# Three reorderings in a two-layer streaming encoder: modulation tiles behind softmax rows, one spread a third of a projection later, one low part ahead of the rotary key

## The reference

```python
for l in range(DEPTH):                                  # DEPTH = 2
    mod = c_act @ w_ada[l] + b_ada[l]                   # 6 * 1024 numbers from the conditioning vector
    sh1, sc1, g1, sh2, sc2, g2 = split(mod, 6)
    h = x * (1.0 + sc1) + sh1
    z = h @ w_in[l]                                     # one projection for four groups of heads
    a_u, a_v, b_cq, b_ckv, b_kr, c_u, d_q, d_f, d_i, d_g = split(z)
    y_a = spatial_gating(gelu(a_u), gelu(a_v), ...)
    y_b = mla(b_cq, b_ckv, b_kr, ...)                   # latent attention, rotary key, 4 heads
    y_c = s5(c_u, ...)                                  # diagonal state-space model
    y_d = hgrn2(d_q, d_f, d_i, d_g, ...)                # gated linear recurrence in chunks of 64
    x = layer_norm(ALPHA * x + (1 + g1) * (rms(y_a..y_d) @ w_out[l]))
    h = x * (1.0 + sc2) + sh2
    x = layer_norm(ALPHA * x + (1 + g2) * conv_ffn(h, ...))   # width 2816, gated, causal conv of 3
```

## Time and profile before

| | us |
|---|---|
| median of 3 runs | 1355.19 |
| lowest, highest | 1354.09, 1362.82 |
| the profiled execution | 1352.38 |
| its span, first to last instruction | 1350.6 |
| mean granted clock of PE, as a share of 2.4 GHz | 0.978 |

### The profile page before, as it was taken

One profiled execution on the slowest core, in us unless ns is written; L12 is line 12 of the kernel. 1 busy time (PEld: TensorE's weight loads), 2 busy tenths in 40 slices (PEclk: granted clock), 3 DMA queues, 4 the chain that ended last, 5 costly groups with the idle time before them and its releaser, 6 DMA issues.

```text
span 1350.6 us, 17196 instructions
## 1 busy us (share of the span) xinstructions
PE 1298.7 (96%) x6802; PEld 1004.0 (74%) x6802; DVE 904.1 (67%) x1537; ACT 532.5 (39%) x796; POOL 243.6 (18%) x201
## 2 busy tenths in 40 slices
PE   6899999999999999999999999999999999999997
PEld 3445767776788888888876677777778888888886
DVE  5985777856877777758657958575675555553335
ACT  2523223533633334434218443443363333343323
POOL 0640200533300000000029432053330000000003
PEclk9998999999999999999989999989999999999998
DMA  9455643122466666755317151122223233333321
GB/s 389 170 125 172 134 152 102 40 66 91 170 189 191 199 194 196 252 203 188 95 61 201 52 96 50 35 87 68 77 91 97 94 94 98 105 95 94 94 94 63
DMA packets 65232, 170.90 MB, mean 127 GB/s; under 512 B 14336, under 2 KB 27008, under 8 KB 64256
## 3 DMA queue, kind: packets, MB, share of 16 engines
q1 hardware_dynamic: 65152, 169.81, 40.3%
HBM read 162.07 MB, written 7.72 MB: 126 GB/s over the span
## 4 chain that ended last, share of the span: by engine, by line
PE 78%; DVE 14%; DMA 2%; issue 2%; POOL 1%; ACT 1%; SPq 0%; ACTq 0%; POOLq 0%; DVEq 0%
PE bank L558 20%; PE bank L560 20%; PE bank L559 20%; PE bank L681 3%; PE bank L708 2%; PE bank L573 1%; PE bank L675 1%; PE bank L567 1%; PE bank L873 1%; PE bank L836 1%; DVE xa L1275 1%; PE bank L578 1%; DVE xa L1281 1%; PE bank L845 1%; DMA cf<-in_consts 1%
## 5 line engine op out<-in xcount | busy, mean ns | idle before, releaser
L558 PE MATMUL bank<-ym_r,scr_r 128*128 128x512 f32 x688 | 268.7, 391 | 6.4 <-DVE hm_r L1942 4.2
L560 PE MATMUL bank<-hm_r,scr_r 128*128 128x512 f32 x688 | 267.8, 389 | 0.0
L559 PE MATMUL bank<-ym_r,ring_r 128*128 128x512 f32 x688 | 267.8, 389 | 0.0
L1344 DVE TENSOR_TENSOR ring_r<-ring,scr_r 128x1024 fp32r<-128x1024 f32 x134 | 165.5, 1235 | 86.1 <-ACT scr_r L2097 85.9
L2097 ACT ACTIVATE scr_r<-ring 128x1024 fp32r<-128x1024 f32 x146 | 153.4, 1052 | 129.5 <-DMA ring<-in_w_down 105.3
L558 PE MATMUL bank<-scr_r 128*128 128x512 f32 x480 | 188.6, 393 | 2.8 <-DVE ym_r L1876 2.8
L559 PE MATMUL bank<-scr_r,ring_r 128*128 128x512 f32 x480 | 187.4, 390 | 0.0
L558 PEld LDWEIGHTS bank<-ym_r,scr_r 128*128 128x128 f32 x688 | 129.1, 188 | 38.2 <-issue 7.8
L560 PEld LDWEIGHTS bank<-hm_r,scr_r 128*128 128x128 f32 x688 | 129.1, 188 | 26.7
L559 PEld LDWEIGHTS bank<-ym_r,ring_r 128*128 128x128 f32 x688 | 129.1, 188 | 26.6
L2438 ACT ACTIVATE scr<-bank,pb 128x512 f32<-128x512 f32 x86 | 67.0, 779 | 194.9 <-PE bank L560 194.9
(11 more groups left out here) (395 smaller groups left out, 2036.9 us busy)
## 6 DMA issues: line engine op xcount, KB each, us to landing
ring<-in_w_up SPq DMA_DIRECT2D x88, 512.0 KB, 3.6
ada<-in_w_ada SPq DMA_DIRECT2D x80, 512.0 KB, 3.6
ring<-in_w_down SPq DMA_DIRECT2D x44, 512.0 KB, 3.5
ring<-in_w_in SPq DMA_DIRECT2D x33, 512.0 KB, 4.3
scr<-in_w_ada SPq DMA_DIRECT2D x16, 512.0 KB, 14.1
ring<-in_w_out SPq DMA_DIRECT2D x16, 512.0 KB, 3.5
pa<-in_par_a SPq DMA_DIRECT2D x2, 2144.5 KB, 12.7
xa<-in_x SPq DMA_DIRECT2D x1, 2048.0 KB, 8.0
```

What stands on the lines that cost most here:

```text
L558: first = mm(dst, w_hi, x_hi, start=start, stop=False)
L559: mm(dst, w_lo, x_hi, start=False, stop=False)
L560: return first, mm(dst, w_hi, x_lo, start=False, stop=stop)
L1344: V.tensor_tensor(ring_r[:, slot(l, n), :], ring[:, slot(l, n), :], high[:, slot(l, n), :].bitcast(F32), ALU.subtract)\
```

## The change

On PE, the spread of the latents' reciprocal roots comes after the last third of F1 rather than before it, in layer 0 only. On DVE, `win_low(l, U1)` moves ahead of the rotary key and the HGRN2 gates; only in layer 1 does it do anything. And 18 of the 24 modulation tiles of layer 0 move: tiles 0 and 1 from ahead of block 0's softmax step to behind the exponents ahead of block 3's, tiles 2 and 3 behind block 3's step, tiles 4 and 5 behind block 4's; tiles 10 to 17 go behind the first level, the states and later blocks. Tiles 6 to 9 and 18 to 23 keep their places. Nothing that is computed changes, and SP's list stays as it is.

```diff
@@ PE @@
                 project(AT[F1], 0)
                 project(AT[F1], 1)
+                if FIRST_SPLIT[l] > 3:
+                    project(AT[F1], 2)
                 pe.wait_ge(S["r_rstd"], l + 1)
                 for r in range(2):
                     for b in range(NB):
                         last = spread(banks[2 + r][:, b * P:(b + 1) * P], 40 + 4 * r + b, P)
                 last.then_inc(S["r_bcast"], 1)
-                project(AT[F1], 2)
+                if FIRST_SPLIT[l] == 3:
+                    project(AT[F1], 2)
@@ DVE @@
                 V.scalar_tensor_tensor(ckv[:, 0, :], ckv[:, 0, :], p_a("kv_norm"), banks[3][:, :], ALU.mult, ALU.mult)\
                     .then_inc(S["r_used"], 1)
+                win_low(l, U1)
...
-                win_low(l, U1)
                 q_rope(0)
...
                 win_low(l, Q0)
-                mods_mix(0)
-                mods_mix(1)
                 attend(0)
...
                 attend(1)
-                mods_mix(2)
-                mods_mix(3)
                 attend(2)
                 win_low(l, Q1)
                 exponent(0)
                 exponent(1)
+                mods_mix(0)
+                mods_mix(1)
                 attend(3)
+                mods_mix(2)
+                mods_mix(3)
+                attend(4)
+                win_low(l, I0)
                 mods_mix(4)
                 mods_mix(5)
-                attend(4)
-                win_low(l, I0)
...
                 s5_out(1)
-                mods_mix(10)
                 v.wait_ge(S["hg_zero"], l + 1)
                 level(0)
-                mods_mix(11)
                 states(0)
                 attend(9)
                 win_low(l, G1)
-                mods_mix(12)
+                mods_mix(10)
                 states(1)
-                mods_mix(13)
+                mods_mix(11)
...
                 level(2)
-                mods_mix(14)
+                mods_mix(12)
                 level(3)
-                mods_mix(15)
+                mods_mix(13)
                 attend(12)
...
                 win_low(l, AV1)
+                mods_mix(14)
+                mods_mix(15)
+                attend(14)
                 mods_mix(16)
-                attend(14)
                 mods_mix(17)
                 s5_skip()
```

## The result

| | before | after |
|---|---|---|
| median of 18 runs each, us | 1355.07 | 1361.34 |
| lowest and highest, us | 1347.12, 1363.30 | 1353.70, 1364.52 |
| profiled execution: time, span, us | 1352.4, 1350.6 | 1364.1, 1362.3 |
| mean clock over the span | 0.978 | 0.973 |

The ratio after to before is 1.0032, interval 1.0016 to 1.0048: the changed kernel is slower by 2 to 7 us. The difference of the medians is 6.3 us.

The account below looks back on a forecast made before the run. PE, busy 1298.7 of 1350.6 us, was taken as the bound. Layer 0's terms, -0.4 + 8.0 + 2.6 - 0.6 - 2.0 - 1.7, with layer 1 at 0, gave +5.9: median 1361.1 us, range 1354 to 1368.

Parts of the forecast that it names:

- The main term: Layer 0, `s5_inputs`: PE waits 8.0 us for the reads of `s5_u`, held back by tiles 4 and 5.
- Edit 1: Layer 0, spread of the latents behind F1's last third: DVE's scaling about 0.4 us later but covered, cost 0.
- Edit 2a: Layer 0, tiles 0 to 3 behind the first softmax rows: gain 0.4 us, rest of that gap and slow clock stay.
- Edit 2b: Layer 0, tiles 4 and 5 behind `attend(4)`: reads of `s5_u` go out late, PE waits 8.0 us at `s5_inputs`.
- The clock: Layer 0, behind the wait at `s5_inputs`: slow clock loses 1.7 or 3.4 us, middle taken, 2.6.
- the third rival: Clock stays low longer behind the wait: three 3.4 us spells lose 5.1, layer 1 may add 1.0; +9.4, chance 0.14.
- Edit 2c: Layer 0, tiles 6 to 17 later: gains 0.6 us at `hg_turn`, 2.0 at `hg_update(0)` and 1.7 of slow clock.
- The 1.7: Layer 0: gain of 1.7 us as the slow spell behind the 2.0 us gap at `hg_update(0)` goes.
- Edit 3: Layer 1, U1's low part before the rotary key: 4.1 us won comes back as waits before Q0, so 0.
- my 0.3: Layer 1: U1's low part may cost 0.3 us more beside GpSimd, given back by work leaving the busy stretch.
- the second, layer 1 keeping its gain: Rival: layer 1 keeps the 4.1 us from U1's earlier low part; +1.8, 1357.0 us, chance 0.08.
- The first, that the reads are there in time: Rival, layer 0: reads of `s5_u` not held back by tiles 4 and 5; -3.3, 1351.9 us, chance 0.12.

Follow-up runs that it names:

- reads first: The changed kernel with SP's loads of tiles 6 and 7 moved in its list behind the eight reads of `s5_u`: 1357.07 us, ratio 1.0012.
- softmax early: The kernel before with DVE's and ScalarE's block 0 softmax ahead of HGRN2's exponentials, DVE's block 1 ahead of tiles 0 and 1: 1354.55 us, ratio 0.9991.
- all four: The kernel before with first softmax steps early, tiles 10 to 17 moved, U1's early low part in layer 1, three SP list entries changed: 1351.36 us, ratio 0.9976.
- second pass: The kernel before with first softmax steps early, tiles 10 to 17 moved, tiles 2 and 3 behind `exponent(1)`, `turned_weights(0)` ahead of the exponentials: 1346.27 us, ratio 0.9926.
- the last: Against second pass: U1's low part ahead of the rotary key, SP's tiles 6, 7 behind `s5_u` reads, 8, 9 behind `s5_k` stores; 1344.96 us, 0.9921 against before.

## Why the prediction was right

It forecast +5.9 us and a median of 1361.1; the runs show +4.3 (2 to 7) by the ratio, and +6.3 by the medians, at 1361.34. The main term, PE's wait for the reads, came in the place, by the chain and at about the size forecast. That the sum comes so close is in part luck, as the steps show:

**Edit 1: 0.** The kernel with the spread alone shows no cost, and its DVE still waits for S5's written weights, 3.45 us where before waited 3.36.

**Edit 2a: -0.4, the gap at 111 stays.** It shrank from 1.4 to 0.9 us (and it is 1.6 in the kernels with the spread or layer 1's low part alone). The forecast had the slow clock behind it stay too. In after there is none, but those two kernels, with the longer gap, show 1.00 there as well: it is not the edit's gain. What I missed is the other half of that move: the slots. In the changed kernel it doesn't show, because tiles 4 and 5 hold the reads back anyway; in the kernel with these two put back it makes a wait of 5.7 us.

**Edit 2b: a wait of 8.0.** It is 8.8, in the place and by the chain forecast. The chain in after, DVE's timeline and SP's issues (they answer to the earlier trace rows):

```profile
133.84 0.56 DVE L1614 TENSOR_REDUCE small<-bank 128x1 f32<-128x384 f32 x1 [9.01 <-PE bank L836]
...
134.96 1.22 DVE L1339 SCALAR_TENSOR_TENSOR ada<-ada,silu_c 128x1024 f32<-128x1024 f32 x1
```

```profile
136.22 1.47 SPq L460 DMA_DIRECT2D ada<-in_w_ada  x2
137.73 0.43 SPq L455 DMA_DIRECT2D ring<-in_w_in  x1
138.26 6.46 SPq L484 DMA_DIRECT2D scr<-s_u  x8
```

Tile 5 follows tile 4 at 136.10. From the scores of block 4 to the first read: 138.26 - 132.99 = 5.3 us, forecast 5.5. From the first read to PE's start: 147.71 - 138.26 = 9.4 us, forecast 8.4. This term was mis-sized. The eight issues took 6.46 us instead of 5.95, and the landing behind them the other half microsecond. PE arrived 5.9 us behind the scores, as forecast. 5.3 + 9.4 - 5.9 = 8.8.

**The clock: 2.6.** Windows of after, the wait's second half, and the stretch behind it, after which the clock is 1.00 again:

```profile
142.80:147.70 4.90, 0.00 (x0) 0.02 (x1) 1.23 (x2) 0.00 (x0) 0.00 (x0) 0.50 0.81 157
147.70:153.00 5.30, 5.29 (x71) 5.18 (x72) 1.51 (x3) 0.00 (x0) 0.00 (x0) 0.50 0.85 268
```

The spell was 10.2 us, as long as the three of 3.4 that the third rival had, but 4.9 us of it fell into the wait, where it costs nothing. Behind it, `s5_inputs` took 3.71 instead of 2.13, and the third of a projection after it 2.82 instead of the 2.05 that such a third takes at full clock: 1.6 + 0.8 = 2.4 us. The term holds. That a slow spell can begin inside the wait was no part of the forecast.

**Edit 2c: -0.6, -2.0, -1.7.** (It names tiles 6 to 17. Of these 6 to 9 keep their places on DVE; in all 14 tiles move, 0 to 5 and 10 to 17, and not 18.) All three are seen in after: no idle time at 162.49 and 174.30 in PE's timeline, no slow spell behind the latter. DVE's scan, which before began 2.4 us behind the end of the transposes, begins 0.13 us behind it (162.49 + 1.04 = 163.53), and DVE now waits for them:

```profile
163.66 2.34 DVE L1710 TENSOR_TENSOR_SCAN ym<-pa,scr 128x512 f32<-128x512 f32 x2 [0.47 <-PE bank L716]
```

My sum was that both causes together (DVE catching up, 2.4, and tile 10 gone, 1.2) exceed 2.0. The experiments show that either is nearly enough alone: tiles 4 and 5 alone removed the wait, and tiles 10 to 17 alone took it down to 0.6. The 1.7 is the weak one: as the section on tiles 10 to 17 shows, the spell follows this gap in some executions only.

Layer 0 in sum: the start of block 4's scores 0.9 earlier, then 8.8 + 2.4 - 0.6 - 2.0 - 1.7 gives 6.0; measured at AV1 5.7, forecast 5.9. But the 0.9 at the start is mostly not the change's. After's lead-in began 1.1 us later; two slow spells of before, at 69 and at 113.5, are missing in after, 1.7 each; the two waits for a turned query, with what follows them, took 1.5 (PE was 0.6 ahead at 84.87, and 0.9 behind at the first scores, 105.25); the gap at 111 is 0.5 shorter and the next 0.3 longer. Forecast were 0.4 of it. The terms that belong to the forecast's sum, 8.8 + 2.4 - 0.5 - 0.6 - 2.0 - 1.7, give 6.4 against its 5.9; the 5.7 at AV1 comes closer by luck.

**Edit 3: 0.** The signature came as forecast: no wait on U1's low part, two others in its place, on a turned query and on Q0's low part. PE's and DVE's timelines of after, layer 1, which answer to the earlier trace rows:

```profile
771.25 0.49 PE L836 MATMUL bank<-scr 128*128 128x128 f32 x2 [0.59 <-DVE scr L1605]
...
776.08 0.50 PE L558 MATMUL bank<-xa_r,ada_r 128*128 128x512 f32 x1 [2.03 <-DVE ring_r L1356]
```

```profile
749.90 2.03 DVE L1356 TENSOR_TENSOR ring_r<-ring,ada_r 128x1024 fp32r<-128x1024 f32 x1
```

The first was 0.6 and not 1.9, the second 2.0 against 2.1. Of the 4.1 us, 2.8 came back and 1.3 was kept up to Q0; in the kernel with this edit alone 2.4 was kept and a slow spell took 1.7 of it. The step that failed in part is "moving an instruction within its list does not shorten the list". DVE's busy time from the latents to Q0 fell from 28.75 to 27.46 us, and that is the 1.3. The instruction itself got dearer: 2.03 us beside POOL, 1.88 in the kernel with this edit alone, where the row of a low part gave 1.20. But the rotary key behind it got cheaper by more, 6.5 us instead of 8.4: its last four instructions took 4.92 us beside a copy of POOL in before, and 2.70 beside a memset of POOL in after.

The Trainium skill, "SBUF — State Buffer", section "SBUF: two separate sides", says that of VectorE and GpSimd the one that starts first has the shared port pair for its whole instruction, and that the other fully blocks; my reading of it was a surcharge of a whole instruction of POOL, 1.3 us. Measured are 0.7 and 0.8: more than my 0.3, less than that. The trace agrees with the page all the same. POOL's timeline of after:

```profile
749.55 1.29 POOL L2547 TENSOR_TENSOR scr<-scr 128x512 f32<-128x512 f32 x1
750.80 2.03 POOL L2555 TENSOR_TENSOR pa<-cf,small 128x512 f32<-128x512 f32 x1
```

When the low part started, at 749.90, POOL's instruction had 0.9 us to go, which is about the surcharge. And POOL's next took 2.03 us, where it took 1.03 in the kernel with edit 3 alone. So what was paid here is the rest of the other's instruction and not a whole one. The sum that I drew from my reading, 1.0 us more for the list, went the wrong way, since the list got shorter.

So of the rivals the second, layer 1 keeping its gain, was right to a third: 4.4 us is 5.7 of layer 0 less 1.3. In the time of the whole kernel this can't be seen (the edit alone: 1.0000 to 1.0042). The first, that the reads are there in time, is refuted by the 8.8 us. The third named a real thing, a longer spell, that cost nothing more.

## What to carry to other kernels

A load that waits for its slot until another engine has used it ties that engine's order to the issuing queue's: before moving such a use, walk the queue's list from the load that waits for it to every transfer behind it, and take the margin of each from the trace. Of several waits, each worth one or two microseconds, removing one here mostly brought up another of about that size close by; look at which wait is second, and time them removed together before dropping the idea. Where a kernel is 96% busy on one engine, cut the spans of two executions at the same pieces of work before explaining their difference: here 7.3 of 11.7 us lay in stretches that nothing had changed, and 1.1 more ahead of the first edit. And trace the same code twice before calling a slow spell the work of an edit.

## What the hardware showed that I had not expected

**The clock falls in some executions and not in others, over the same code.** The kernel before shows 6.8 us at 0.51 behind the narrow matmuls of `s5_kernels`, without a gap. The window from 121 to 136 us holds that stretch in each of the twelve traces. The mean granted clock there is 0.77 in seven (before, after, tiles 4 and 5 alone, reads first, softmax early, tiles 10 to 17, all four) and 1.00 in four (tiles 4 and 5 back, layer 1 alone, spread alone, second pass), with 0.89 in the last. The spread alone and layer 1 alone do the same work there as the kernel before. Half speed for 6.8 us is 3.4 us: the size of the effects sought here, and it may be one reason for the spread of 16 us over 18 runs of the kernel before. Likewise the spell at 113.5 of before is absent in after, though gaps of 0.9 and 1.3 us remain; one at about 70 us is in six of the twelve traces; and the one behind the gap of 2.0 us is in before and with layer 1's low part alone, but not with the spread alone. With layer 0 unchanged, these spells and the waits that come in their place moved AV1 by 4.6 us.

**Eight reads into `us` cost the issuing queue 3.8 to 6.5 us,** for the same bytes: 5.95 before, 6.46 in after, 3.77 and 3.76 in the kernels with tiles 4 and 5 back and with the reads first. It is 3.94 with layer 1's low part alone, where layer 0 is that of before, so the order of the lists alone doesn't set it. In the three traces where no tile loads stand just ahead of the reads it is 3.76 each time; behind tile loads it ran from 3.77 to 6.54. What makes the difference wasn't tried.
